# Expert weights in transfers of two units, 16 KB on a partition, over a ring of six pairs

## The chip, the core and the metric

The kernel runs on one core of one Trainium2 chip. What is measured is the device time of one execution in microseconds (us). Three runs of the kernel before took 1349.79, 1351.2 and 1353.6 us, a median of 1351.2 us.

## The reference

A decoder layer for 512 prompt tokens and 8 sample tokens. Its head (attention with a sliding window, a pooling mixer, a projection, norms) gives rows h of 1024 numbers. Its tail is a mixture of 32 experts, of which each token uses 4. Everything is float32.

```
logits = h @ w_router + b_router;  topv, topi = top_k(logits, 4);  gates = softmax(topv)
for every expert e and the tokens that chose it:
    gu = h[tok] @ w1[e] + b1[e]              # w1[e]: 1024 x 2048
    gate, up = gu[:, :1024], gu[:, 1024:]
    gate = min(gate, 7);  up = clip(up, -7, 7)
    act = (up + 1) * (gate * sigmoid(1.702 * gate))
    y[tok] += g * (act @ w2[e] + b2[e])      # w2[e]: 1024 x 1024
out = x + gate_ffn * y
```

An expert has 12 MB of weights (w1 8 MB, w2 4 MB), all 32 have 384 MB, and all are read from HBM once.

## The kernel before

The first 300 us are the head. After it come 32 passes, one expert each. `ORDER` gives every pass a class: A takes up to 256 token rows, B 128, C 64, D 32. The order is CCBBCBDDADDBBCCDADCBDDADCBCBCBDD: 3 passes of A, 9 of B, 9 of C and 11 of D. Experts with most rows get class A, and so on down. All passes read the same 12 MB whatever their class; what differs is the work of TensorE. In A and B it multiplies in three terms (`three`), for which ScalarE first makes a high part (`hi`, L2059) and VectorE a low part (`rawr`, L2242) of each half of a unit.

The weights of a pass are cut into 12 *units* of 1 MB, 8 KB on each of 128 partitions. Units 0 to 7 are w1, in which unit u holds rows 128u to 128u + 127; units 8 to 11 are w2, in which a unit holds 256 rows, two neighbouring rows on a partition. TensorE uses the units in the order of `pe_order()`: w1 of pass p, then w2 of pass p - 1 (in A these four stand between unit 3 and unit 4). Below, (p, u) is unit u of pass p. `unit_used` counts units that TensorE is done with, and each unit's place in that count is `USED`.

SyncE (SP) issues all weight transfers, one or two DMAs to a unit (two for w1 of A, whose halves of 512 columns are needed at different times; they have pieces of 2 KB). They go into `m.raw`, a ring of 13 slots of 1 MB (`RING`). Slots are handed on in the order of use: the transfer of a unit waits until the unit 13 places before it is used (`FREED`, `SLOT`), and it signals its slot's semaphore `raw_in`, on which TensorE (C, D) or ScalarE (A, B) waits. SP works strictly in order:

```
                if n >= RING:
                    sp.wait_ge(unit_used, USED[FREED[n - RING]])
                m.load_unit(sp, e[p], p, u)
```

At the start the 12 units of pass 0 and unit (1, 0) fill the ring while the head still runs, and units (1, 1) to (1, 4) go to four other buffers (`EARLY`), lent by tiles that are used later.

The rows of a pass come by an indirect DMA of GpSimd (POOL) and are turned on TensorE (`turn_x`, L2446): the transpose of columns 128k to 128k + 127 gives the left operand of unit k. The activations are turned by `turn_act` (L2470), with columns in steps of 2 (8 bytes), since a w2 unit has two neighbouring rows on a partition. The outputs of a pass go out by two indirect DMAs of POOL that add to HBM (yd at L1918, out_y_prompt at L1935); with more than one block of rows (A) there are four. Each waits for the one before of its kind.

Of the kernel before, what the change touches and what calls it, by code (L numbers as in the profile page):

```python
# [21 lines left out]
P = 128  # L22
# [78 lines left out]

def arrivals():

    total, at = [0] * RING, {}
    for unit in LOADS:
        total[SLOT[unit]] += 16 * unit_dmas(*unit)
        at[unit] = total[SLOT[unit]]
    return at, total
# [23 lines left out]
def build(nc, i, o):  # L132
    m = Record()
    m.i, m.o = i, o
    with ExitStack() as ctx:
# [162 lines left out]
        def et(name, shape, dt=F32):  # L298
# [23 lines left out]
                   for n, place in enumerate((aTl0, xTl0, hi0 + SLOT_B, hi0))}  # L322
        m.aTh = et("aTh", [P, 2 * KC, P], F32R)
# [52 lines left out]
def head(nc, m):  # L376
# [160 lines left out]

    def load_unit(sp, e, p, u):

        if (p, u) in EARLY:  # L540
            raw, landed = m.early[p, u][:], m.early_in
        else:
            raw, landed = m.raw[:, SLOT[p, u], :], m.raw_in[SLOT[p, u]]
        if u >= W1_UNITS:
            f = 2 * (u - W1_UNITS)
            src = w2[ds(e), f * P:(f + 2) * P, :].rearrange("e (p k) n -> p (e k n)", k=2)
            sp.dma_start(raw, src).then_inc(landed, 16)
        elif ORDER[p] == "A":
            j = u // 4
            for kk in range(2):  # L550
                k = 2 * (u % 4) + kk
                src = w1[ds(e), k * P:(k + 1) * P, :].rearrange("e p (h c) -> p (e h) c", h=2)
                sp.dma_start(raw[:, kk * D:(kk + 1) * D].rearrange("p (h c) -> p h c", h=2),  # L553
                             src[:, :, j * 512:(j + 1) * 512]).then_inc(landed, 16)
        else:
            src = w1[ds(e), u * P:(u + 1) * P, :].rearrange("e p n -> p (e n)")
            sp.dma_start(raw, src).then_inc(landed, 16)

    m.load_unit = load_unit
# [1153 lines left out]
def experts(nc, m):  # L1713
# [107 lines left out]
    with nc.Block() as block:  # L1821

        @block.sync
        def _(sp):
# [179 lines left out]
        def _(act):  # L2004
# [43 lines left out]
            def high_to(place):  # L2048

                while high_count[0] < len(SPLIT_UNITS) and USED[SPLIT_UNITS[high_count[0]]] <= place:  # L2050
                    n = high_count[0]
                    slot = SLOT[SPLIT_UNITS[n]]
                    act.wait_ge(m.raw_in[slot], ARRIVED[SPLIT_UNITS[n]])
# [364 lines left out]
        def _(pe):  # L2418
# [42 lines left out]
            def turn_act(c, h, before, lows):  # L2461
# [41 lines left out]
            def up_unit(c, u, raw, xT):  # L2503

                final = u == W1_UNITS - 1
# [3 lines left out]
                elif c == "C":  # L2509
                    for sec in range(2):  # L2510
                        for h in range(2):
                            last = mm(bank[sec][64 * h:64 * h + 64, :], xT[:, u % 4, 64 * (u // 4):64 * (u // 4) + 64],
                                      raw[:, D * sec + 512 * h:D * sec + 512 * h + 512], stop=final)
# [58 lines left out]
            def up_static(p, u):  # L2572
                if ORDER[p] in SPLIT:
                    split_unit(p, u)
                elif (p, u) in EARLY:
                    pe.wait_ge(m.early_in, len(EARLY) * 16)
                    up_unit(ORDER[p], u, m.early[p, u][:], m.xT[p % 2])
                else:
                    slot = SLOT[p, u]
                    pe.wait_ge(m.raw_in[slot], ARRIVED[p, u])  # L2580
                    up_unit(ORDER[p], u, m.raw[:, slot, :], m.xT[p % 2])

            def down(p):
# [7 lines left out]
                for u in range(W1_UNITS, UNITS):  # L2591
                    if c in SPLIT:
                        split_unit(p, u)
                    else:
                        slot = SLOT[p, u]
                        pe.wait_ge(m.raw_in[slot], ARRIVED[p, u])
# [168 lines left out]
```

## Time and profile before

| what | us |
|---|---|
| median of three runs | 1351.2 |
| the profiled execution, its own time | 1354.14 |
| its span, first to last instruction | 1352.6 |
| TensorE busy | 1218.1 |
| VectorE busy | 713.6 |
| ScalarE busy | 489.6 |
| GpSimd busy | 326.7 |
| mean granted clock of TensorE | 0.945 |

Times within the execution count from the start of its span. Busy time of TensorE is modelled: matmuls are pipelined, so "busy" is not "at its peak". The rows of the DMA engines are in the page's slices of 34 us each and in windows that are asked for; a share of 1.0 means that all 16 DMA engines moved packets all the time (a little over 1 can show where packets of one engine overlap). The time from the issue of a transfer to its landing contains its wait behind the transfers ahead of it in the queue.

### The profile page before, as it was taken

To read this page: it belongs to the slowest core of one execution; us is meant where nothing else is said; L and a number is where in the kernel's file an instruction comes from. 1 tells how busy PE (TensorE), PEld (TensorE's weight loads), DVE (VectorE), ACT (ScalarE), POOL (GpSimd) and SP (SyncE) were. 2 spreads that over 40 slices of the span, in tenths; PEclk is the share of its full clock that TensorE was granted. 3 is DMA by queue.
4 is the path that set the end of the run, shared out by engine and by line. 5 is a ranking of instruction groups with operands and counts; after the bars stand their busy time and mean duration, and the time that the engine had idled before them with its cause. 6 is when DMAs were issued, how large, how long until landed. Compare 5 with 4: busy or idle time off the path is not lost.

```text
span 1352.6 us, 17632 instructions
## 1 busy us (share of the span) xinstructions
PE 1218.1 (90%) x6408; PEld 725.9 (54%) x6408; DVE 713.6 (53%) x1118; ACT 489.6 (36%) x703; POOL 326.7 (24%) x353
## 2 busy tenths in 40 slices
PE   5899799969999979998899889998889998999973
PEld 2455455553675735755675247555457555565531
DVE  3532663463785874553794234546534536667530
ACT  5111432231564633332573133333323333546320
POOL 2232221031222213113322311143321133232111
PEclk9899799979999989999899999998979998999976
DMA  9950786489999999999999999999999999999993
GB/s 332 345 127 5 263 302 215 158 316 385 400 391 363 406 408 393 404 385 371 402 414 407 398 397 407 388 363 402 403 393 408 359 345 408 413 407 412 403 413 113
DMA packets 101404, 474.16 MB, mean 351 GB/s; under 512 B 17417, under 2 KB 19896, under 8 KB 55162
## 3 DMA queue, kind: packets, MB, share of 16 engines
q1 hardware_dynamic: 82282, 444.76, 82.2%
q0 software_dynamic: 18384, 26.53, 8.0%
q10 hardware_dynamic: 650, 1.72, 0.4%
q8 instruction: 52, 0.85, 0.3%
q14 instruction: 36, 0.29, 0.1%
HBM read 459.47 MB, written 32.66 MB: 364 GB/s over the span
## 4 chain that ended last, share of the span: by engine, by line
PE 53%; DMA 12%; DVE 6%; issue 4%; ACT 1%; POOL 1%; SPq 0%; POOLq 0%; DVEq 0%; ACTq 0%
PE bank L2422 51%; DMA raw<-in_w 5%; DVE rawr L2242 2%; DMA out_y_prompt<-gu,slot_tok 2%; DMA yd<-gu,idx_s 2%; DMA yd<-ost,idx_s 2%; PE bank L2470 1%; PE bank L2446 1%; ACT hi L2059 1%; POOL gu L1932 1%; DVE gu L2206 1%; DVE gu L2204 0%; DVE ost L2276 0%; ACT ost L2042 0%; SPq L553 0%
## 5 line engine op out<-in xcount | busy, mean ns | idle before, releaser
L2242 DVE TENSOR_TENSOR rawr<-raw,hi 128x1024 fp32r<-128x1024 f32 x288 | 351.6, 1263 | 106.3 <-ACT hi L2059 104.8
L2059 ACT CAST hi<-raw 128x1024 fp32r<-128x1024 f32 x288 | 294.8, 1048 | 166.1 <-PE bank L2422 140.9
L2422 PE MATMUL bank<-raw,xT_even 128*64 128x512 f32 (+1 forms) x704 | 135.2, 600 | 0.1
L1918 POOL DMA_INDIRECT yd<-ost,idx_s x31 | 56.5, 1824 | 325.4 <-ACT ost L2042 324.5
L2422 PE MATMUL bank<-raw,aT 128*32 128x256 f32 (+1 forms) x992 | 113.7, 478 | 11.5 <-DMA raw<-in_w 11.5
L2422 PE MATMUL bank<-raw,xT_odd 128*32 128x512 f32 (+1 forms) x544 | 84.8, 647 | 15.8 <-DMA raw<-in_w 15.8
L2422 PE MATMUL bank<-hi,xTh_odd 128*128 128x512 f32 x224 | 76.8, 426 | 19.8 <-DVE rawr L2242 19.5
L2422 PE MATMUL bank<-hi,aTh 128*128 128x512 f32 x240 | 77.3, 404 | 12.5 <-DVE rawr L2242 12.5
L2422 PE MATMUL bank<-hi,xTh_even 128*128 128x512 f32 x256 | 84.5, 412 | 3.9 <-DVE rawr L2242 3.8
L2204 DVE TENSOR_SCALAR gu<-bank 128x512 f32<-128x512 f32 (+1 forms) x50 | 31.4, 627 | 103.2 <-PE bank L2422 103.2
L2024 ACT ACTIVATE gu<-gu 128x512 f32<-128x512 f32 (+1 forms) x50 | 29.2, 583 | 145.6 <-DVE gu L2204 145.6
L2422 PEld LDWEIGHTS bank<-raw,aT 128*32 128x32 f32 (+1 forms) x992 | 42.2, 125 | 73.1 <-issue 40.6
L2422 PE MATMUL bank<-rawr,xTh_even 128*128 128x512 f32 x256 | 80.8, 397 | 0.0
L2422 PE MATMUL bank<-hi,xTl_even 128*128 128x512 f32 x256 | 80.8, 397 | 0.0
L1869 POOL DMA_DIRECT2D bt<-bd x32 | 18.6, 583 | 238.1 <-PE bank L2422 214.9
L2422 PE MATMUL bank<-hi,aTl 128*128 128x512 f32 x240 | 76.0, 399 | 0.0
L2422 PE MATMUL bank<-rawr,aTh 128*128 128x512 f32 x240 | 76.0, 399 | 0.0
L2422 PE MATMUL bank<-rawr,xTh_odd 128*128 128x512 f32 x224 | 72.7, 407 | 0.0
L2422 PE MATMUL bank<-hi,xTl_odd 128*128 128x512 f32 x224 | 72.0, 404 | 0.0
L2042 ACT ACTIVATE ost<-bank,slot_gate 128x512 f32<-128x512 f32 (+1 forms) x43 | 26.0, 634 | 123.9 <-PE bank L2422 112.1
L1935 POOL DMA_INDIRECT out_y_prompt<-ost,slot_tok x20 | 33.3, 1666 | 146.0 <-DVE ost L2276 143.2
L2422 PEld LDWEIGHTS bank<-raw,xT_even 128*64 128x64 f32 (+1 forms) x704 | 35.4, 126 | 60.4 <-issue 57.8
(387 smaller groups left out, 1847.6 us busy)
## 6 DMA issues: line engine op xcount, KB each, us to landing
raw<-in_w SPq DMA_DIRECT2D x356, 1024.0 KB, 14.7
raw<-in_w SPq DMA_DIRECT2D x48, 512.0 KB, 13.1
raw<-in_w_ada SPq DMA_DIRECT2D x21, 1024.0 KB, 7.7
w_in_sb<-in_w_in SPq DMA_DIRECT2D x4, 1280.0 KB, 16.2
w_out_sb<-in_w_out SPq DMA_DIRECT2D x4, 1024.0 KB, 9.0
early<-in_w SPq DMA_DIRECT2D x4, 1024.0 KB, 12.4
ada_more<-in_w_ada SPq DMA_DIRECT2D x3, 1024.0 KB, 13.8
xs<-in_x_prompt SPq DMA_DIRECT2D x4, 512.0 KB, 14.1
```

The costliest lines, as they stand in the source:

```text
L1869: gp.dma_start(m.bt[0:rows, buf, :], table[ds(e), :, :].rearrange("e r c -> (e r) c")).then_inc(bias_in[buf], 16)
L1918: gp.indirect_dma_start(yd_of[n], bass.IndirectOffsetOnAxis(ap=m.idx_s[:, p % 6, b:b + 1], axis=0), out_rows(p, b), None, bounds_check=lim ...
L1932: gp.tensor_tensor(scaled_rows(p, b)[rows, cols], out_rows(p, b)[rows, cols], g, ALU.mult).then_inc(wide_scaled, 1)
L1935: gp.indirect_dma_start(y_of[n], bass.IndirectOffsetOnAxis(ap=m.slot_tok[:, p % 6, b:b + 1], axis=0), scaled_rows(p, b), None, bounds_chec ...
L2024: nc.scalar.activation(gate, gate, ACT.Silu, scale=ALPHA).then_inc(silu_ready, 1)
L2042: done = nc.scalar.activation(out_rows(p, b)[:, n * w:(n + 1) * w], src, ACT.Copy, scale=m.slot_gate[:, p % 6, b:b + 1])
L2059: nc.scalar.copy(m.hi[:, (2 * n + h) % HI, :], m.raw[:, slot, h * D:(h + 1) * D]).then_inc(hi_done, 1)
L2204: v.tensor_scalar(gate, g, LIMIT, None, ALU.min).then_inc(gmin_ready, 1)
L2206: v.tensor_scalar(up, u, LIMIT, -LIMIT, ALU.min, ALU.max).then_inc(gu_free, 1)
L2242: v.tensor_tensor(m.rawr[slot][:, half], m.raw[:, slot, half], m.hi[:, (2 * n + h) % HI, :].bitcast(F32), ALU.subtract).then_inc(lo_done, 1)
L2422: return nc.tensor.matmul(out, lhsT, rhs, start=start, stop=stop, skip_group_check=True)
L2446: last = tr(bank[6][:, n * P:(n + 1) * P], xg[:, b, (k + n) * P:(k + n + 1) * P], m.ident[:])
```

## The change

Two neighbouring units make a pair, 2 MB, 16 KB on a partition. In most cases one DMA brings a pair. What moves:

- **Layout.** Partition p of a w1 pair holds rows 2p and 2p + 1 of its 256 rows, next to each other in HBM: one piece of 16 KB. A w2 pair of A, B and C holds rows 4p to 4p + 3 of its 512 rows, one piece of 16 KB. A w2 pair of D is one DMA of two pieces of 8 KB for each partition. The w1 units of A stay two DMAs each, in pieces of 2 KB.
- **Ring.** Pairs go round six pairs of slots, 0 to 11. Slot 12 holds unit (1, 0) once and is not used again. A pair waits until the *second* unit of the pair six places before it is used.
- **Landing.** One DMA has one semaphore, so both units of a pair wait for the whole pair (`LAND`).
- **Start.** Pass 0 and unit (1, 0) are loaded as single units, with the new layout. Unit (1, 5) becomes a fifth early unit, in two tiles of 4 KB.
- **Turns.** `turn_x` takes columns in steps of 2 (8 bytes) in place of neighbours; `turn_act` takes steps of 4 (16 bytes) in A, B and C, and stays at 2 in D.

The core of the diff:

```diff
-EARLY = [(1, u) for u in range(1, 5)]
-LOADS = [(0, u) for u in range(UNITS)] + [unit for unit in pe_order() if unit[0] and unit not in EARLY]
-FREED = [unit for unit in pe_order() if unit not in EARLY]
-SLOT = {unit: n for n, unit in enumerate(LOADS[:RING])}
-for after, unit in zip(FREED, LOADS[RING:]):
-    SLOT[unit] = SLOT[after]
+EARLY = [(1, u) for u in range(1, 6)]
+SINGLE = [(0, u) for u in range(UNITS)] + [(1, 0)]
+SLOT = {unit: n for n, unit in enumerate(SINGLE)}
+HELD = [(p, u) for p, u in pe_order() if not u % 2 and (p != 1 or u >= 6)]
+PAIRS = [unit for unit in HELD if unit[0]]
+FREED = {}
+for (q, w), (p, u) in zip(HELD, PAIRS):
+    FREED[p, u] = (q, w + 1)
+    SLOT[p, u], SLOT[p, u + 1] = SLOT[q, w], SLOT[q, w + 1]
...
+def one_transfer(p, u):
+    return ORDER[p] != "A" or u >= W1_UNITS
...
+    def load_pair(sp, e, p, u):
+        if not one_transfer(p, u):
+            load_unit(sp, e, p, u)
+            load_unit(sp, e, p, u + 1)
+            return
+        n = SLOT[p, u]
+        raw = m.raw[:, n:n + 2, :]
+        if u < W1_UNITS:
+            src = w1_pair(e, u // 2).rearrange("e (p k) n -> p (e k) n", k=2)
+        elif ORDER[p] == "D":
+            f = 2 * (u - W1_UNITS)
+            src = w2[ds(e), f * P:(f + 4) * P, :].rearrange("e (i p k) n -> p (e i) (k n)", i=2, k=2)
+        else:
+            src = w2_pair(e, (u - W1_UNITS) // 2).rearrange("e (p i k) n -> p (e i) (k n)", i=2, k=2)
...
+        sp.dma_start(raw, src).then_inc(m.raw_in[LAND[p, u]], 16)
...
-            for n in range(UNITS + 1, len(LOADS)):
-                p, u = LOADS[n]
+            for p, u in PAIRS:
...
-                if n >= RING:
-                    sp.wait_ge(unit_used, USED[FREED[n - RING]])
-                m.load_unit(sp, e[p], p, u)
+                sp.wait_ge(unit_used, USED[FREED[p, u]])
+                m.load_pair(sp, e[p], p, u)
...
-                    last = tr(bank[6][:, n * P:(n + 1) * P], xg[:, b, (k + n) * P:(k + n + 1) * P], m.ident[:])
+                    first = (k + n) // 2 * 2 * P
+                    last = tr(bank[6][:, n * P:(n + 1) * P], xg[:, b, first + n % 2:first + 2 * P:2], m.ident[:])
...
-                    first = 2 * P * (n // 2)
-                    last = tr(bank[7][:, n * P:(n + 1) * P], up[:, first + n % 2:first + 2 * P:2], m.ident[:])
+                    columns = up[:, n:2 * P:2] if c == "D" else up[:, n:4 * P:4]
+                    last = tr(bank[7][:, n * P:(n + 1) * P], columns, m.ident[:])
```

SP's order around the point where the w2 units of pass 9 end and the weights of pass 11 begin (`eid` holds the number of the expert; L547 and L557 are `load_unit`). The order names a semaphore by its first user in the program, so "bada_in" is `unit_used` here. Before:

```order
L547 ISA [waits bada_in]
L547 DMA raw_79<-in_w2 128x2048
L547 ISA [waits bada_in]
L547 DMA raw_79<-in_w2 128x2048
L1835 TENSOR_LOAD eid_210
L1835 ISA x2
L557 ISA [waits bada_in]
L557 DMA raw_79<-in_w1 128x2048
L557 ISA [waits bada_in]
L557 DMA raw_79<-in_w1 128x2048
```

And now, where L615 is `load_pair`:

```order
L615 ISA [waits bada_in]
L615 DMA raw_79<-in_w2 128x2x2048
L1893 TENSOR_LOAD eid_212
L1893 ISA x2
L615 ISA [waits bada_in]
L615 DMA raw_79<-in_w1 128x4096
```

One wait and one DMA stand where there were two of each; nothing changes its place among the passes.

TensorE's order in pass 15 (D), where its first w1 units are used (L2422 is `mm`, L2470 `turn_act`; `raw_in` is the landing of a slot). Before:

```order
L2422 MATMUL bank0<-raw_79,xT_odd_184 32x512 [waits raw_in3,vecs_in,us_tr]
L2422 MATMUL bank0<-raw_79,xT_odd_184 32x512 x3
L2422 MATMUL bank0<-raw_79,xT_odd_184 32x512 [waits raw_in4]
L2422 MATMUL bank0<-raw_79,xT_odd_184 32x512 x3
L2470 MATMUL bank7<-ident_49,gu_185 128x128 [waits gate_in,recip_ready,us_rows]
L2470 MATMUL bank7<-ident_49,gu_185 128x128 x3
L2422 MATMUL bank0<-raw_79,xT_odd_184 32x512 [waits raw_in5]
```

And now (L2479 and L2528 are the same two):

```order
L2479 MATMUL bank0<-raw_79,xT_odd_184 32x512 [waits raw_in2,vecs_in,us_tr]
L2479 MATMUL bank0<-raw_79,xT_odd_184 32x512 x3
L2479 MATMUL bank0<-raw_79,xT_odd_184 32x512 [waits raw_in2]
L2479 MATMUL bank0<-raw_79,xT_odd_184 32x512 x3
L2528 MATMUL bank7<-ident_49,gu_185 128x128 [waits gate_in,recip_ready,us_rows]
L2528 MATMUL bank7<-ident_49,gu_185 128x128 x3
L2479 MATMUL bank0<-raw_79,xT_odd_184 32x512 [waits raw_in4]
```

The instructions stand where they stood. What differs is that two units in a row wait for one landing.

## Rows read from the trace of the kernel before

**Rows 1.** The page: DMA engines in 40 slices of the span.
```profile
DMA  9950786489999999999999999999999999999993
GB/s 332 345 127 5 263 302 215 158 316 385 400 391 363 406 408 393 404 385 371 402 414 407 398 397 407 388 363 402 403 393 408 359 345 408 413 407 412 403 413 113
```

**Rows 2.** The waits of the whole span: us in total, times, longest us.
```profile
PEld bank L2422 <- DMA raw<-in_w: 46.1, 28, 4.7
```

**Rows 3.** The page, DMA issues: KB each, median us to landing.
```profile
raw<-in_w SPq DMA_DIRECT2D x356, 1024.0 KB, 14.7
```

**Rows 4.** The waits, 767 to 793 us.
```profile
PEld bank L2422 <- DMA raw<-in_w: 11.9, 8, 2.0
```

**Rows 5.** The waits, 970 to 995 us.
```profile
PEld bank L2422 <- DMA raw<-in_w: 13.3, 8, 2.5
```

**Rows 6.** The waits, 1303 to 1337 us.
```profile
PEld bank L2422 <- DMA raw<-in_w: 20.4, 11, 4.7
```

**Rows 7.** Windows: busy PE, PEld, DVE, ACT, POOL; clock, DMA share, GB/s.
```profile
610.00:620.00 10.00, 10.00 (x52) 6.74 (x50) 0.00 (x0) 2.07 (x4) 0.53 (x1) 1.00 0.84 318
880.00:890.00 10.00, 10.00 (x45) 5.34 (x45) 0.00 (x0) 2.81 (x5) 4.11 (x3) 1.00 0.83 323
...
1080.00:1090.00 10.00, 10.00 (x45) 7.71 (x45) 0.59 (x1) 0.73 (x2) 0.00 (x0) 1.00 0.78 314
760.00:770.00 10.00, 10.00 (x68) 3.09 (x62) 1.97 (x7) 1.28 (x2) 3.52 (x4) 1.00 1.02 420
```

**Rows 8.** SP's issues in time, 862 to 893 us: start, length, count.
```profile
868.00 11.32 SPq L547 DMA_DIRECT2D raw<-in_w  x3
884.49 6.88 SPq L557 DMA_DIRECT2D raw<-in_w  x4
```

**Rows 9.** Line L557, 884 to 886.5 us: from issue to landing.
```profile
DMA to landing us min/median/max: 5.0/5.0/5.0
```

**Rows 10.** Line L557, 748 to 757 us: from issue to landing.
```profile
DMA to landing us min/median/max: 20.4/20.6/24.0
```

**Rows 11.** DMA, 1290 to 1296 us: packets, MB, share of 16 engines.
```profile
DMA packets 352, 2.56 MB, mean 427 GB/s; under 512 B 39, under 2 KB 39, under 8 KB 39
...
q1 hardware_dynamic: 352, 2.56, 101.1%
```

**Rows 12.** DMA, 815 to 819 us.
```profile
DMA packets 693, 1.64 MB, mean 409 GB/s; under 512 B 44, under 2 KB 44, under 8 KB 643
...
q1 hardware_dynamic: 692, 1.63, 106.0%
```

**Rows 13.** DMA, 72 to 79.5 us.
```profile
q0 software_dynamic: 571, 1.45, 85.2%
q1 hardware_dynamic: 18, 0.15, 10.2%
```

**Rows 14.** TensorE in time, 773 to 800 us: start, length, operation, wait before.
```profile
777.07 1.06 PE L2422 MATMUL bank<-raw,xT_odd 128*32 128x512 f32 x8 [1.72 <-DMA raw<-in_w]
...
790.48 1.94 PE L2422 MATMUL bank<-raw,aT 128*64 128x512 f32 x8 [0.40 <-DMA raw<-in_w]
```

**Rows 15.** TensorE in time, 1300 to 1353 us: its last unit.
```profile
1335.59 1.07 PE L2422 MATMUL bank<-raw,aT 128*32 128x256 f32 x16 [0.91 <-DMA raw<-in_w]
```

**Rows 16.** Line L2446, turns of rows: ns min/median/max of one.
```profile
L2446 PEld LDWEIGHTS bank<-ident,xg_even x100: 137/141/223, 300.4 to 1258.7; 128*128 128x128 f32 x100
```

**Rows 17.** Line L2470, turns of activations.
```profile
L2470 PEld LDWEIGHTS bank<-ident,gu x178: 194/207/219, 322.8 to 1327.3; 128*128 128x128 f32 x178
```

**Rows 18.** ScalarE in time, 631 to 642 us.
```profile
640.91 0.47 ACT L2042 ACTIVATE ost<-bank,slot_gate 128x256 f32<-128x256 f32 x1 [7.97 <-POOL gu L1932]
```

**Rows 19.** The DMA view, issues of POOL: median us to landing.
```profile
out_y_prompt<-ost,slot_tok POOLq DMA_INDIRECT x20, 8.9
```

More of the change, by code:

```diff
@@ L99, in unit_dmas @@
     return 2 if u < W1_UNITS and ORDER[p] == "A" else 1
+def one_transfer(p, u):
+    return ORDER[p] != "A" or u >= W1_UNITS
+LAND = {unit: n for n, unit in enumerate(SINGLE)}
+for p, u in PAIRS:
+    LAND[p, u], LAND[p, u + 1] = SLOT[p, u], SLOT[p, u if one_transfer(p, u) else u + 1]
 def arrivals():
     total, at = [0] * RING, {}
-    for unit in LOADS:
-        total[SLOT[unit]] += 16 * unit_dmas(*unit)
-        at[unit] = total[SLOT[unit]]
+    for unit in SINGLE:
+        total[LAND[unit]] += 16 * unit_dmas(*unit)
+        at[unit] = total[LAND[unit]]
+    for p, u in PAIRS:
+        if one_transfer(p, u):
+            total[LAND[p, u]] += 16
+            at[p, u] = at[p, u + 1] = total[LAND[p, u]]
+        else:
+            for unit in ((p, u), (p, u + 1)):
+                total[LAND[unit]] += 16 * unit_dmas(*unit)
+                at[unit] = total[LAND[unit]]
     return at, total
@@ L322, in build @@
                    for n, place in enumerate((aTl0, xTl0, hi0 + SLOT_B, hi0))}
+        m.early[EARLY[4]] = [at(f"early4_{n}", [P, D], F32, place) for n, place in enumerate((x0 + 4096, aT0 + 4096))]
         m.aTh = et("aTh", [P, 2 * KC, P], F32R)
@@ L536, in tok, with w1_pair, w2_pair @@
         return slice(t * P, t * P + ROWS[t])
+    def w1_pair(e, j):
+        return w1[ds(e), 2 * j * P:2 * (j + 1) * P, :]
+    def w2_pair(e, j):
+        return w2[ds(e), 4 * j * P:4 * (j + 1) * P, :]
     def load_unit(sp, e, p, u):
+        j, one = u // 2 if u < W1_UNITS else (u - W1_UNITS) // 2, u % 2
+        if (p, u) == EARLY[4]:
+            for sec in range(2):
+                src = w1_pair(e, j).rearrange("e (p k) n -> p (e k) n", k=2)[:, one, sec * D:(sec + 1) * D]
+                sp.dma_start(m.early[p, u][sec][:], src).then_inc(m.early_in, 16)
+            return
         if (p, u) in EARLY:
@@ L542, in load_unit @@
         else:
-            raw, landed = m.raw[:, SLOT[p, u], :], m.raw_in[SLOT[p, u]]
-        if u >= W1_UNITS:
+            raw, landed = m.raw[:, SLOT[p, u], :], m.raw_in[LAND[p, u]]
+        if u >= W1_UNITS and ORDER[p] == "D":
             f = 2 * (u - W1_UNITS)
@@ L1829, in _ @@
             e = list(range(NE))
-            for n in range(UNITS + 1, len(LOADS)):
-                p, u = LOADS[n]
+            for p, u in PAIRS:
                 if p == PINNED and not u:
@@ L2052, in high_to @@
                     slot = SLOT[SPLIT_UNITS[n]]
-                    act.wait_ge(m.raw_in[slot], ARRIVED[SPLIT_UNITS[n]])
+                    act.wait_ge(m.raw_in[LAND[SPLIT_UNITS[n]]], ARRIVED[SPLIT_UNITS[n]])
                     for h in range(2):
@@ L2501, in down_bias, with up_unit @@
                 last.then_inc(bias_used, 1)
-            def up_unit(c, u, raw, xT):
+            def up_unit(c, u, raw, xT, halves=None):
+                if c == "C" and halves is None:
+                    halves = [raw[:, 0:D], raw[:, D:2 * D]]
                 final = u == W1_UNITS - 1
@@ L2512, in up_unit @@
                             last = mm(bank[sec][64 * h:64 * h + 64, :], xT[:, u % 4, 64 * (u // 4):64 * (u // 4) + 64],
-                                      raw[:, D * sec + 512 * h:D * sec + 512 * h + 512], stop=final)
+                                      halves[sec][:, 512 * h:512 * h + 512], stop=final)
                 else:
@@ L2575, in up_static @@
                 elif (p, u) in EARLY:
-                    pe.wait_ge(m.early_in, len(EARLY) * 16)
-                    up_unit(ORDER[p], u, m.early[p, u][:], m.xT[p % 2])
+                    pe.wait_ge(m.early_in, EARLY_LANDED)
+                    tiles = m.early[p, u]
+                    halves = [t[:] for t in tiles] if u == EARLY[4][1] else [tiles[:, 0:D], tiles[:, D:2 * D]]
+                    up_unit(ORDER[p], u, None, m.xT[p % 2], halves)
                 else:
                     slot = SLOT[p, u]
-                    pe.wait_ge(m.raw_in[slot], ARRIVED[p, u])
+                    pe.wait_ge(m.raw_in[LAND[p, u]], ARRIVED[p, u])
                     up_unit(ORDER[p], u, m.raw[:, slot, :], m.xT[p % 2])
@@ L2595, in down @@
                         slot = SLOT[p, u]
-                        pe.wait_ge(m.raw_in[slot], ARRIVED[p, u])
+                        pe.wait_ge(m.raw_in[LAND[p, u]], ARRIVED[p, u])
                         down_unit(c, u, slot)
```

18 lines of the change are left out of this document (13 added, 5 removed).

## The prediction

> **What bounds the kernel now.** I read the page's slices first. From 306 us on, after the head, the DMA engines are busy in nine tenths or more of nearly every slice, at 345 to 414 GB/s [rows 1]. The 32 passes have to bring 384 MB (402.7 million bytes). So the passes are close to the rate of the DMA engines, and TensorE's 90% of busy time is not the whole story. The question is when TensorE waits for a weight and when the weights wait for a slot.
>
> The waits answer it. TensorE's weight loads wait 46.1 us for expert weights in the whole span [rows 2], although a transfer is issued well ahead: 14.7 us pass in the median until it lands [rows 3]. By windows, 11.9 us of it lie in 767:793, 13.3 us in 970:995 and 20.4 us in 1303:1337 [rows 4 to 6], so nearly all of it in three stretches. In 777 us the wait stands before every unit [rows 14]. In between the weights are ahead. The windows of 10 us show the opposite state: at 610, 880 and 1080 us the DMA share falls to 0.84, 0.83 and 0.78, while TensorE is busy for the whole 10 us [rows 7]. These are the w2 units of the three A passes. A unit of A takes TensorE 5.5 us (the three issues from 868.00 on stand 5.5 us apart, then comes one at 884.49 [rows 8]) and a transfer far less, so the ring is full and the DMA engines stand idle. The time to landing says the same: 5.0 us for the transfer issued at 884.5, with nothing ahead of it in the queue [rows 9], and 20.4 us and more for those at 748 to 757, with several MB ahead of them [rows 10].
>
> So the tail is three cycles of one form. TensorE is the bound until the ring is last full (618, 884 and 1089 us, each time the end of an A pass); from there the DMA engines are the bound: TensorE uses up what is ahead, runs dry (near 770, 970 and 1303 us) and stays dry until the next A pass, or the end. In this part of a cycle TensorE's work is hidden, and two things count: how long the bytes take, and how far ahead the transfers were when the ring was last full.
>
> **The change part by part.**
>
> *Bytes in pieces of 16 KB.* The number of bytes stays. Between 1290 and 1296 us SP's queue moved 352 packets, 39 of them tiny (completions) and 313 of 8 KB, in 101.1% of 16 x 6.0 us, which is 97.1 us [rows 11]: 0.310 us for 8 KB with its share of the completions. Between 815 and 819 us it moved 692 packets in 106.0% of 16 x 4.0 us, 67.8 us; of them 44 are tiny, 599 have 2 KB and 49 have 8 KB [rows 12]. Less 49 x 0.310 us that leaves 52.6 us, 0.088 us for 2 KB. From 2 to 8 KB a packet grows by 0.222 us, so 8 KB more cost 0.296 us, and 16 KB would be 0.606 us against 2 x 0.310 us. Each engine has 8 partitions, so a pair costs 8 x 0.014 = 0.11 us less of some 4.96 us (2.2%). This counts only where DMA is the bound. In use order the last full moments lie at the issues of units number 128, 224 and 296, and the dry stretches end at 187, 259 and 383, so 60, 36 and 88 units lie between. Less the w2 units of D (4, 4 and 8), which keep pieces of 8 KB, that is 168 units or 84 pairs: 84 x 0.11 = -9.4 us. The bounds: nothing (16 KB cost just two of 8 KB), and 149 pairs in all of the tail x 0.11 = -16.4 us.
>
> The Trainium skill has a rule for this part (SBUF — State Buffer, "The DMA setup-cost knee"): a transfer pays about 2 us whatever its size, so a load that is bound by DMA should be merged into the largest transfers one can. By its formula (2 us + bytes / 436 GB/s) 1 MB takes 4.4 us and two units in one 6.8 us in place of 8.8; taken one after the other, 84 pairs would give back 168 us. The trace does not bear out that this cost is paid one transfer after the other: with several queued the engines moved 427 GB/s, 2.48 us to a unit [rows 11].
>
> *The ring, 12 slots in place of 13, freed two at a time.* When TensorE ended the A unit at 884.3 us, the transfer that could start was that of the unit 13 places later; all before it had landed or were nearly there. Now the last A unit is the second of its pair, and what its end frees is the pair six places later: units 11 and 12 places on. At the same moment the transfers are two units behind. That is the same at 618 and 1089 us, since all three are the end of unit (p, 11) of an A pass. Two units are 2 x 8 x 0.310 = 4.96 us of the DMA engines, and from there they are the bound, so nothing hides it: 3 x 4.96 = +14.9 us. It also adds up, since after each dry stretch TensorE is the bound and starts later. Bounds: one unit only for each cycle (+7.4 us) if a slot's reuse was late anyway, and three units (+22 us) if SP's wait for the second unit leaves a further hole. I take two, which the positions give.
>
> *Landing of pairs.* In a dry stretch TensorE now waits for 2 MB and then has two units to do. While it is dry that is hidden by the next transfer. At its end it is not: after the last landing two units stand before the end of the stretch, not one. A unit took 1.06 us at 777 us, 1.94 us at 790 us (the lower clock) and 1.07 us as the last of all [rows 14, 15]; I take 1.5 us, three times: +4.5 us (bounds 3 and 6).
>
> *SP.* It issues half as many DMAs and nothing changes place. Queued behind a waiting pair are only later pairs; no other queue is passed. Nothing.
>
> *Start.* Unit (1, 5) comes early, the first pairs of pass 2 come about when they did and the next ones some us later. No wait for weights before 767 us has any size (the three stretches hold 45.6 of the 46.1 us), so the cover is a deep one and I count nothing; if that cover were gone it would be one unit, 2.5 us.
>
> *Turns.* A weight load that turns neighbouring columns takes 141 ns, one with steps of 8 bytes 207 ns [rows 16, 17]. 178 loads of rows go from the first to the second: 178 x 66 ns = 11.7 us if all of it showed. Loads run beside matmuls and about half the tail is bound by DMA, so I take +1 us for all turns. The 16-byte step of 156 loads is not in the trace; by the nearest rows it lies between no change and twice 207 ns (0 to +32 us, or a little below nothing if the step does not matter). I take it as small, nearest to the step from 141 to 207 in a matmul stream that hides it. The Trainium skill (SBUF — State Buffer, "Door 1: The DMA port swizzle") says that SBUF has lines of 16 bytes and wants two hits or more in each. By that rule steps of 16 bytes, one hit in each line, are slower than steps of 8; the trace has only the two smaller steps, and already the one of 8 bytes costs 66 ns.
>
> **The sum.** -9.4 + 14.9 + 4.5 + 1 = +11.0 us, which I round down to +10, since a part of the extra idle time of the DMA engines lets POOL's transfers through, which they would have to carry anyway. On the profiled execution's own 1354.1 us that is 1364; it lies 2.9 us above the median of the runs, and on that median, 1351.2 us, the forecast is 1361 us.
>
> **The rivals.**
>
> *Larger pieces win.* The mechanism: the DMA engines are the bound all through, as the slices seem to say [rows 1], and the ring's last unit is never missed. Then the whole -16.4 us comes: 1335 us. For it speaks a share of 1.02 even at 760 us; against it the full ring at 610, 880 and 1080 us [rows 7]. The point from which it decides: the two lost units would have to cost under 1.5 us a cycle. The rule on merged transfers above points this way. Chance 0.15.
>
> *The two cancel.* The ring costs one unit a cycle: -9.4 + 7.4 + 3 = +1 us, 1352 us. Chance 0.15.
>
> *POOL's transfers get stuck behind large pieces.* At 640.9 us ScalarE had waited 7.97 us for the rows of an A pass to go out, and a store takes 8.9 us to land [rows 18, 19]. Its rows of 4 KB are 8 for an engine; if each waits for one weight packet, that packet grows from 0.31 to 0.61 us, +2.4 us for a store and +9.6 us for the four in a row after an A pass. That moves TensorE's stalls, and mostly where DMA is the bound and hides them; if all of it showed, 3 x 9.6 = +29 us beside the forecast's 10: 1390 us. Chance 0.07. That the engines take turns between queues by packets is what the Trainium skill says (DMA: Bandwidth & Descriptors, "Queues, rings and completion order").
>
> *Pieces of 16 KB are slow, or strides are.* Between 72 and 79.5 us SP's queue moved a load with 9 rows of 16 KB in 10.2% of 16 x 7.5 us: 1.36 us each, beside POOL's 85% [rows 13]. Were that the rate of such pieces alone, 149 pairs x 8 x 0.74 us = +880 us, 2230 us; I give it 0.01, since only the shared engines explain it as well. A piece 5% longer than forecast (0.636 us) gives 84 x 8 x 0.03 = +20 us beside the forecast's 10, 1381 us; the strides' full cost (+32 us) would give some 1392 us. Chance of these 0.07.
>
> **How the numbers follow.** Forecast 0.55, and the rivals 0.15, 0.15, 0.07 and 0.08. The range of the forecast itself, by the bounds of its ring and landing, is 1350 to 1369; to hold 8 in 10 it reaches toward the cases on both sides: 1344 to 1376 us. About 0.3% (4 us) is what a measurement can tell from no change. Faster by more: the first rival and a little of the second, 0.16. Within: the rest of the second and the low edge of the forecast, 0.16. Slower: 0.68.
>
> **What would show it.** Right: packets of 16 KB at about 0.606 us in a full stretch, near 430 GB/s; DMA shares below 0.8 at 610, 880 and 1080 us, lower than before; TensorE dry earlier than 767 and 970 us, with fewer and longer waits; about 5 us later at the first A pass after a dry stretch, about 8 at the next, 10 at the end. Wrong: no deeper idle of the DMA engines at the three full moments; or a rate in full stretches outside 420 to 435 GB/s; or new waits of TensorE for ScalarE or VectorE behind POOL's stores, or weight loads of L2528 well above 207 ns.

## The result, and the profile after

The changed kernel takes 1366.4 us in the median of 5 runs (1358.97 to 1369.26), the kernel before 1351.2: the ratio is 1.010, 95% interval [1.0067, 1.0133]. The forecast was 1361 us, its range 1344 to 1376. The profiled execution took 1358.97 us by its own time, the fastest of the five; its span is 1357.3 us at a mean granted clock of 0.951.

The page of the changed kernel, SP's queue and issues (packets, MB, share of 16 engines; then count, KB each, median us to landing), answers to [rows 3]:

```profile
q1 hardware_dynamic: 60618, 444.75, 81.3%
...
raw<-in_w SPq DMA_DIRECT2D x171, 2048.0 KB, 13.3
```

Of before the same row of the page is:

```profile
q1 hardware_dynamic: 82282, 444.76, 82.2%
```

The bytes are the same. The packets took 81.3% of 1357.3 us = 1103.5 us where they had taken 82.2% of 1352.6 = 1111.8 us.

The windows of the changed kernel (busy PE, PEld, DVE, ACT, POOL; clock, DMA share, GB/s), against [rows 7]:

```profile
610.00:620.00 10.00, 10.00 (x67) 4.87 (x65) 1.71 (x5) 2.80 (x5) 4.13 (x3) 1.00 0.69 256
...
880.00:890.00 10.00, 10.00 (x45) 6.46 (x46) 0.00 (x0) 2.42 (x4) 1.78 (x2) 1.00 0.53 183
...
1090.00:1100.00 10.00, 10.00 (x48) 4.14 (x48) 0.84 (x6) 2.80 (x5) 5.77 (x4) 1.00 0.73 256
```

At the end of each A pass the DMA engines stand idle longer than before: 0.69, 0.53 and 0.73 where it was 0.84, 0.83 and 0.78 (the third window lies 10 us later). A window of 10 us can cut such a hole in two, so these shares show that the holes are deeper and not by how many us.

The waits of TensorE's weight loads over the whole span of the changed kernel (us in total, times, longest):

```profile
PEld bank L2479 <- DVE rawr L2299: 56.1, 30, 10.4
PEld bank L2479 <- DMA raw<-in_w: 35.4, 13, 4.2
```

and of the kernel before, the row that [rows 2] does not show:

```profile
PEld bank L2422 <- DVE rawr L2242: 41.9, 27, 10.0
```

The wait for weights fell from 46.1 us in 28 waits to 35.4 in 13: fewer, and longer in the mean (1.6 to 2.7 us). That is not the whole wait for weights: in passes of A and B ScalarE takes them first (`hi`), and it waited 25.1 us in 8 waits before and 28.9 us in 12 in the changed kernel. The wait for VectorE's low parts rose by 14.2 us, of which 13.5 us lie behind the three A passes (14.7, 11.0 and 9.4 us in place of 10.0, 5.6 and 6.0). There it begins on POOL. These are the waits of POOL, of before, of the change and of the changed kernel with 8 KB pieces (e1_pieces8, below):

```profile
POOL gu L1932 <- DMA yd<-gu,idx_s: 26.7, 3, 9.5
```

```profile
POOL gu L1989 <- DMA yd<-gu,idx_s: 39.3, 3, 14.9
```

```profile
POOL gu L1983 <- DMA yd<-gu,idx_s: 26.9, 3, 10.1
```

POOL's second product of an A pass waits for its store; ScalarE waits for POOL, VectorE for ScalarE, TensorE for VectorE. In the changed kernel ScalarE's row that answers to [rows 18] is

```profile
643.24 0.47 ACT L2099 ACTIVATE ost<-bank,slot_gate 128x256 f32<-128x256 f32 x1 [11.47 <-POOL gu L1989]
```

11.47 us in place of 7.97. And the stores' landings (median us), against [rows 19]:

```profile
yd<-ost,idx_s POOLq DMA_INDIRECT x31, 10.9
...
out_y_prompt<-ost,slot_tok POOLq DMA_INDIRECT x20, 11.8
```

So a store takes 2.4 us more (8.5 before) and 2.9 us more (8.9 before). That is the third rival's mechanism, and it is real: behind the A passes TensorE's stalls are longer by it. Whether it costs time at the end is for the experiments.

Where the 13.5 us (1.0% of 1351.2) arise can be read from the semaphore on which TensorE counts units. From the first unit on (it is done at 303.8 us in the profiled run of before, at 296.8 in that of the change, and anywhere from 295 to 304 in the others, so spans alone mislead) the changed kernel is late, in us, after so many units:

```
units used           16   112   144   184   208   240   256   280   352   383
changed - before   +2.1  +3.5  +9.3 +11.5  +9.4 +14.4 +17.6  +9.9 +14.9 +13.9
12 slots - before   0.0  +2.4  +2.6  +6.6  +9.1  +9.7 +11.7 +12.4 +13.0 +14.8
```

(the second row is e3_ring12, below). The changed kernel jumps by about 5 us behind each A pass (units 112 to 144, 208 to 240, 280 to 352), where TensorE waits for VectorE, and gets a part back in the next dry stretch. The kernel that differs only in its ring gains nothing back. Each row is one execution: that of the change was the fastest of its five, that of e3 the slowest of its six, so the steps of a row say more than its end. In the dry stretches (184, 256, 383) the numbers also move by up to 3 us from one unit to the next, since the units of a pair land together.

### The profile page after: what moved, and what is told of

It is laid out like the page before. It is cut to its first block, busy times and chain, and to the rows that moved or that the text cites. A ratio compares the mean times of both kernels' runs of the same rounds, so it can differ in the third digit from the quotient of the medians.

```text
span 1357.3 us, 17126 instructions
## 1 busy us (share of the span) xinstructions
PE 1211.5 (89%) x6408; PEld 728.9 (54%) x6408; DVE 708.6 (52%) x1118; ACT 488.8 (36%) x703; POOL 322.4 (24%) x353
## 3 DMA queue, kind: packets, MB, share of 16 engines
q1 hardware_dynamic: 60618, 444.75, 81.3%
q10 hardware_dynamic: 650, 1.72, 0.4%
## 4 chain that ended last, share of the span: by engine, by line
PE 52%; DMA 14%; DVE 6%; issue 4%; ACT 1%; POOL 1%; POOLq 0%; SPq 0%; DVEq 0%; ACTq 0%
PE bank L2479 49%; DMA raw<-in_w 6%; DMA yd<-gu,idx_s 3%; DMA out_y_prompt<-gu,slot_tok 3%; DVE rawr L2299 3%; DMA yd<-ost,idx_s 2%; PE bank L2528 1%; PE bank L2504 1%; ACT hi L2116 1%; POOL gu L1989 1%; DVE gu L2263 1%; DVE gu L2261 0%; DVE ost L2333 0%; ACT ost L2099 0%; DMA out_y_prompt<-ost,slot_tok 0%
## 5 line engine op out<-in xcount | busy, mean ns | idle before, releaser
L2299 DVE TENSOR_TENSOR rawr<-raw,hi 128x1024 fp32r<-128x1024 f32 x288 | 347.3, 1250 | 115.7 <-ACT hi L2116 114.2
L2479 PE MATMUL bank<-raw,xT_even 128*64 128x512 f32 (+1 forms) x704 | 135.3, 600 | 0.1
L2479 PE MATMUL bank<-raw,aT 128*32 128x256 f32 (+1 forms) x992 | 113.9, 482 | 16.1 <-DMA raw<-in_w 16.1
L2479 PE MATMUL bank<-hi,xTh_odd 128*128 128x512 f32 x224 | 76.8, 426 | 34.1 <-DVE rawr L2299 34.1
L2479 PE MATMUL bank<-raw,xT_odd 128*32 128x512 f32 (+1 forms) x536 | 80.6, 631 | 11.4 <-DMA raw<-in_w 11.4
L2479 PE MATMUL bank<-hi,aTh 128*128 128x512 f32 x240 | 77.4, 404 | 12.7 <-DVE rawr L2299 12.7
L2479 PE MATMUL bank<-hi,xTh_even 128*128 128x512 f32 x256 | 82.5, 404 | 2.9 <-DVE rawr L2299 2.9
L2479 PEld LDWEIGHTS bank<-raw,aT 128*32 128x32 f32 (+1 forms) x992 | 43.7, 127 | 76.1 <-issue 44.5
L2479 PE MATMUL bank<-hi,xTl_even 128*128 128x512 f32 x256 | 79.6, 392 | 0.0
L2479 PE MATMUL bank<-rawr,xTh_even 128*128 128x512 f32 x256 | 79.6, 392 | 0.0
L2479 PE MATMUL bank<-rawr,aTh 128*128 128x512 f32 x240 | 75.5, 396 | 0.0
L2479 PE MATMUL bank<-hi,aTl 128*128 128x512 f32 x240 | 75.3, 395 | 0.0
L2479 PE MATMUL bank<-rawr,xTh_odd 128*128 128x512 f32 x224 | 72.6, 406 | 0.0
L2479 PE MATMUL bank<-hi,xTl_odd 128*128 128x512 f32 x224 | 72.5, 406 | 0.0
L2479 PEld LDWEIGHTS bank<-raw,xT_even 128*64 128x64 f32 (+1 forms) x704 | 35.4, 126 | 59.6 <-issue 54.9
```

The costliest lines, as they stand in the source:

```text
L2299: v.tensor_tensor(m.rawr[slot][:, half], m.raw[:, slot, half], m.hi[:, (2 * n + h) % HI, :].bitcast(F32), ALU.subtract).then_inc(lo_done, 1)
L2479: return nc.tensor.matmul(out, lhsT, rhs, start=start, stop=stop, skip_group_check=True)
```

## The experiments

Four kernels ran on each of three chips, each beside its own runs of the kernel before (medians 1349.8, 1351.55 and 1351.8 us). Ratios are against those; where two kernels of different chips are compared, their ratios are, and the intervals are combined as if independent.

**The change taken apart.** *e1_pieces8* keeps pairs, ring and joint landing, but moves every pair in pieces of 8 KB, with the layout and turns of before.

```
- src = w1_pair(e, u // 2).rearrange("e (p k) n -> p (e k) n", k=2)
+ src = w1[ds(e), u * P:(u + 2) * P, :].rearrange("e (i p) n -> p (e i) n", i=2)
```

> The changed kernel's ring, pairs, one DMA and one landing for a pair, but with the old layout: a pair comes in two pieces of 8 KB on a partition in place of one of 16 KB, and the turns take the columns as before. Theory 1 (the ring: transfers stand two units behind at each full moment): nothing of that changes, only the small gain of 16 KB pieces is lost, 84 x 8 x 7 ns = 5 us, so 1369 to 1373 us; the store of yd after pass 10 still holds GpSimd for 11 us. Theory 2 (POOL's stores wait behind pieces twice as long and hold ScalarE and then TensorE): the wait of GpSimd for the store of yd goes back from 11.3 to about 8.2 us, the step of 5 us in pass 11 disappears, and the time falls to 1352 to 1360 us.

1368.0 us, ratio 1.012 [1.0093, 1.0147]. That is 1 us below theory 1's range and far above theory 2's. POOL's wait is back at 26.9 us (the row above), its stores land in 8.5 us, and the kernel is not faster for it. So the stores' longer landing alone does not explain the loss; what may take its place here is said at e7.

*e2_two_dmas* is the changed kernel with each pair as two DMAs with a semaphore each.

```
- return ORDER[p] != "A" or u >= W1_UNITS
+ return False
```

> The changed kernel with its layout, turns and ring of six pairs, but every pair comes as two DMAs with a semaphore each (pieces of 8 KB). Against the run with 8 KB pieces in one DMA it differs in the landing alone. Theory 1: the ring's loss stays, the landing of pairs (my 4.5 us) goes away: 1361 to 1368 us. Theory 2: stores are short again and the ring costs little: 1351 to 1357 us.

1374.0 us, ratio 1.0189 [1.0163, 1.0215]: slower by more than any theory said. The two units of a pair land apart, TensorE waits 53.6 us in 33 waits, and the time is 9 us above e1's (from which it also differs by the layout and the turns, free by e4 below). So landing jointly costs nothing that shows here; why two DMAs for a pair cost more than one of the same pieces stays open.

*e3_ring12* is the kernel before with the 13th slot never used again; units are freed singly.

```
- FREED = [unit for unit in pe_order() if unit not in EARLY]
+ FREED = [unit for unit in pe_order() if unit not in EARLY and unit != (1, 0)]
```

> The kernel before with a ring of 12 slots in place of 13, freed one at a time (slot 12 holds unit (1, 0) once). Theory 1: one unit less at each of three full moments, 3 x 2.5 us: 1357 to 1360 us. Theory 2: the ring's length does not matter by itself, 1350 to 1353 us.

1362.4 us, ratio 1.0079 [1.0055, 1.0102], 10.7 us: above what was expected. One slot alone costs as much as three quarters of the change's loss. Its lateness begins at unit 92, long before the first dry stretch that the waits of TensorE had shown. There the first A pass begins, and it is ScalarE that waits. The first of its waits (2.8 us in three; the kernel before has none between 515 and 625 us), and TensorE's window 585:590 of before and of e3:

```profile
528.13 1.99 ACT L2059 CAST hi<-raw 128x1024 fp32r<-128x1024 f32 x2 [1.56 <-DMA raw<-in_w]
```

```profile
585.00:590.00 5.00, 5.00 (x38) 1.50 (x31) 2.19 (x9) 0.60 (x1) 2.31 (x4) 0.80 0.87 313
```

```profile
585.00:590.00 5.00, 5.00 (x25) 1.53 (x28) 2.05 (x5) 0.16 (x1) 1.90 (x3) 0.50 0.62 218
```

By the wait 1.1 us are lost at unit 92. The other 1.3 us are lost at units 104 to 106 with no wait: behind a short idle of TensorE that both kernels have, its granted clock is at the lower level (0.50, 1.2 GHz) for 6.8 us in e3, from 583.9 us on, and for 3.4 us in the kernel before.

*e4_layout* is the kernel before with the changed layout of weights and the turns by column steps.

```
- last = tr(..., xg[:, b, (k + n) * P:(k + n + 1) * P], m.ident[:])
+ last = tr(..., xg[:, b, first + n % 2:first + 2 * P:2], m.ident[:])
```

> The kernel before (13 single slots) with the changed kernel's layout of the weights (8 KB pieces at a pitch of 16 KB in HBM) and its turns with column steps of 2 and 4. Both theories: no change, 1350 to 1354 us. If the turns or the pitch carried a part of the loss it would be 1356 us or more.

1350.8 us, ratio 1.0012 [0.9992, 1.0031]: no change. The turn of activations in the changed kernel (ns min/median/max; the step is now 16 bytes for most), against [rows 17]:

```profile
L2528 PEld LDWEIGHTS bank<-ident,gu x178: 194/211/231, 317.6 to 1331.4; 128*128 128x128 f32 x178
```

**The ring against the pieces.** *e5_ring13_pairs* puts the 13th slot back and keeps 16 KB pieces wherever two slots are neighbours; *e8_ring13_pieces8* is the same with 8 KB pieces and the old layout; *e6_ring11* takes one slot more away; *e7_single_at_A* frees singly at the end of A passes.

```
e5:  for after, unit in zip(HELD, LATER):
         FREED[unit] = after
         SLOT[unit] = SLOT[after]
     ... one_transfer: SLOT[p, u + 1] == SLOT[p, u] + 1 and ...
e6:  - if unit not in EARLY]
     + if unit not in EARLY + [(1, 0), (0, 11)]]
e7:  if ORDER[q] == "A" and w >= W1_UNITS:
         for one in range(2):
             sp.wait_ge(unit_used, USED[q, w - 1 + one])
             m.load_unit(sp, e[p], p, u + one)
```

> Ring of 13 slots as in the kernel before, and 16 KB pieces: a pair goes as one transfer wherever its two slots are neighbours and it has 16 KB pieces (103 of 183 pairs); the other units go singly, each when its own slot is free. Theory 1 (what made the change slower is the lost slot and the freeing by twos at the full moments): a pair that waits for a slot 13 places back is issued at the end of an even unit, so next to nothing is missing at the full moments; the time is that of before less the gain of the larger pieces in the dry stretches, 0.11 us x about 47 pairs (103/183 of 84) = 5 us, plus at most 4.5 us of landing: 1345 to 1351 us, at least 10 us below the changed kernel. Theory 2 (large pieces cost as much as they give: stores of POOL land 2 to 3 us later, a pair lands later than its first unit): no gain from the ring, 1357 to 1366 us.

1353.8 us, ratio 1.0026 [1.0004, 1.0047]. With 13 slots, and pairs freed 13 places back, three quarters of the loss are gone, which theory 2 excludes; but the time lies 3 us above theory 1's range, so the pieces' 5 us, less the landing, did not come. Of all these kernels that keep the computation whole none beats the kernel before.

> The same issue order, pairs and ring of 13 as the run with 13 slots and 16 KB pieces, but every transfer in 8 KB pieces and the weights laid out as before. Theory 1 (a 16 KB piece is 0.014 us shorter than two of 8 KB, and this shows only in the dry stretches): 3 to 6 us above that run, 1350 to 1356 us. Theory 2 (a large piece gives nothing or less, since stores wait behind it): equal to that run within 2 us or below it.

1356.7 us, ratio 1.003 [1.0004, 1.0056]: against e5 0.04% more by the ratios (give or take 0.34%, 5 us), 2.9 us by the medians, too little to tell from none. The store of yd lands in 8.4 us here and in 10.1 us in e5.

> The kernel before with a ring of 11 single slots (the loads of the 12th and 13th slot are never followed by another), 8 KB pieces and single freeing as before. With 12 slots the ratio was 1.0079 [1.0055, 1.0102], 10.7 us. Theory 1 (each slot is a unit of head start lost at the full moments, linear): twice that, 1368 to 1374 us. Theory 1b (the first lost slot cost more than the prediction's 2.48 us a cycle for a reason of its own, and each further one costs 3 x 2.48 us): 1366 to 1369 us. Theory 2 (the last slots are spare, the loss with 12 slots was noise of the start): 1355 to 1362 us.

1375.5 us, ratio 1.0176 [1.0139, 1.0213], 23.8 us. The second slot costs 13 us, the first cost 10.7: linear, as theory 1 has it, and a little above its range.

> The changed kernel (12 slots, 16 KB pieces), but the two pairs that wait for the w2 units of an A pass (six pairs in all) go as single units, each when its own slot is free. Theory 1 (freeing by twos costs one unit at each of three full moments): 3 x 2.48 = 7.4 us less than the changed kernel, 1356 to 1361 us. Theory 2 (freeing by twos costs nothing, only the lost slot and the pieces do): within 2 us of the changed kernel, 1364 to 1368 us.

1363.2 us, ratio 1.0092 [1.0056, 1.0128]: 1 us below the changed kernel by the ratios, 3 by the medians, outside the range of either theory. The interval of the difference is some 7 us to either side, so the total alone just reaches the 7.4 of theory 1. Yet the hole at the end of the first A pass did close. The windows of e7_single_at_A show where it went:

```profile
610.00:620.00 10.00, 10.00 (x68) 4.92 (x67) 1.94 (x6) 2.81 (x5) 4.18 (x3) 1.00 0.95 369
660.00:670.00 10.00, 9.48 (x42) 7.55 (x41) 6.57 (x8) 5.16 (x6) 0.26 (x1) 0.91 0.86 305
...
880.00:890.00 10.00, 10.00 (x46) 6.45 (x46) 0.00 (x0) 2.42 (x4) 1.72 (x2) 1.00 0.77 296
920.00:930.00 10.00, 2.13 (x10) 1.41 (x8) 3.36 (x11) 2.33 (x3) 3.15 (x3) 0.73 1.03 404
930.00:940.00 10.00, 9.63 (x34) 7.79 (x35) 9.16 (x9) 4.47 (x5) 3.39 (x4) 0.76 0.89 326
```

The DMA share is 0.95 at 610 and 0.77 at 880 us (0.69 and 0.53 in the changed kernel). But then TensorE stands still behind POOL's stores (busy for 2.13 us in 920:930, 1.88 in 1130:1140), the transfers run on and fill the ring, and the share falls to 0.85 to 0.89 afterwards. The ring is last full there, not at the end of the A pass, and whatever was behind has been made up. The changed kernel has this second hole too (0.88 in 930:940, 0.89 in 1140:1150). The same window in it and in e1_pieces8:

```profile
930.00:940.00 10.00, 8.61 (x32) 7.04 (x33) 9.65 (x9) 4.40 (x5) 4.42 (x4) 0.76 0.88 353
```

```profile
930.00:940.00 10.00, 9.46 (x36) 7.70 (x37) 9.79 (x9) 4.49 (x5) 3.56 (x4) 0.83 1.03 407
```

The kernels with 8 KB pieces (before, e1, e3, e8) stall there as well, for less long, and have no second hole: their share stays at 1.01 or more. In e5, with 16 KB pieces and 13 slots, it is 0.94. So it takes the longer stall that the 16 KB pieces bring to fill the ring. In the changed kernel the stores' stall is paid and the freeing by twos hides beneath it; in e1 the stores are short and the freeing by twos can show, within the 5.5 us (give or take 5) that e1 lies above e3, which hold the landing and the start as well. That may be why e1 and the changed kernel take the same time. It is read from the shares; no run has the longer stall without the 16 KB pieces.

**Without the stall.** This reading was tested by leaving the stores of the A passes out, in four kernels: before, changed, e7's and e3's.

```
- gp.indirect_dma_start(yd_of[n], ...)
+ if c != "A":
+     gp.indirect_dma_start(yd_of[n], ...)
  ...
+ if c == "A":
+     continue
  gp.indirect_dma_start(y_of[n], ...)
```

(the waits on the two stores' semaphores count the remaining ones).

> The kernel before without the four stores that POOL issues for each of the three A passes (twelve in all; those rows are not added to the outputs). ScalarE then waits only for POOL's two products, and TensorE no longer stands still for 8 to 10 us after each A pass. All theories: faster than before, up to 3 x 9 us where TensorE is the bound, but the DMA engines are the bound behind it, so 5 to 20 us: 1330 to 1346 us. It is the base for the three runs beside it.

1335.9 us, ratio 0.9895 [0.9864, 0.9925]: 14.2 us faster than before.

> The kernel before with 12 single slots, without those twelve stores. Theory 1 (a lost slot is 2.48 us in each of four dry stretches, with or without the stall): 8 to 12 us above the kernel before without the stores. Theory 2 (the stall, during which the ring runs full, is what makes a slot cost 10.7 us and not 7.4): 4 to 7 us above it.

1349.0 us, 0.9988 [0.9966, 1.001]: 12.6 us above e9 by the ratios. A slot costs as much without the stall (a little over theory 1's range), and theory 2 falls, by little: the interval of the difference reaches from 7.5 to 18 us.

> The changed kernel with the same twelve stores left out. Theory 1 (in the changed kernel the hole that freeing by twos leaves at the end of an A pass is filled again while TensorE stands still behind POOL's stores; without the stores the hole stays open): the distance to the kernel before without those stores grows from 13.6 us to 17 to 22 us (7.4 for the slot, 7.4 for the twos, 4.5 landing, less 5 for the pieces, and a fourth dry stretch). Theory 2 (the stores' longer landing, 2 to 3 us each, is a part of the loss): the distance shrinks to 5 to 11 us. Theory 3 (stores and stall play no part): 11 to 16 us as with the stores.

1348.0 us, 0.9984 [0.9961, 1.0006]: 12.0 us above e9. The distance did not grow as theory 1 had it; by the total, theory 3 fits best, but the interval, 7 to 17 us, leaves the upper part of theory 2's range open. The parts moved, though:

> The changed kernel without those twelve stores, and with the six pairs that wait for w2 units of A passes sent as single units. With the stores this step gave 1 us at most. Theory 1 (the stall hid it): now it gives back the prediction's 3 x 2.48 = 7.4 us (5 to 9 us) against the changed kernel without the stores. Theory 3 (freeing by twos costs nothing whatever the stall): within 2 us of it.

1344.2 us, 0.9939 [0.9918, 0.9961]: 6.1 us below e10 by the ratios (3.8 by the medians; the intervals just meet), where the same edit with the stores gave 1 (3 by the medians). The two differ by 5 us, give or take 8, so the totals alone do not show that the stall hides the hole; the shares do. The windows of e11_single_no_stores and of e10_after_no_stores in the stretch behind the third A pass show no stall and no second hole:

```profile
1080.00:1090.00 10.00, 10.00 (x45) 4.90 (x43) 0.00 (x0) 2.80 (x5) 4.78 (x4) 1.00 0.79 292
...
1140.00:1150.00 10.00, 10.00 (x53) 3.86 (x51) 2.47 (x9) 1.78 (x3) 2.98 (x4) 1.00 1.01 412
```

```profile
1080.00:1090.00 10.00, 10.00 (x48) 3.94 (x49) 0.85 (x6) 2.80 (x5) 5.60 (x7) 1.00 0.74 251
...
1140.00:1150.00 10.00, 10.00 (x53) 3.90 (x51) 3.65 (x10) 2.06 (x4) 1.09 (x2) 1.00 1.01 402
```

The lateness by units against e9 (read as the table above):

```
units used           16    88   112   144   184   208   256   280   352   383
e12, 12 slots      +0.2   0.0  +2.3  +2.3  +5.8  +6.4  +9.4  +8.0  +8.0 +11.0
e10, changed       +2.4  +3.3  +7.1 +10.4 +13.4  +6.5 +13.1  +7.3  +7.9 +11.5
e11, singly at A   +2.4  +3.3  +7.0  +7.5  +9.1  +5.3 +11.6  +4.0  +4.6  +7.4
```

e12 loses 2.3, 4.1, 1.6 and 3.0 us in four places: the three dry stretches, and one at units 88 to 112. Against e11, e10 is 2.9 us later once the first A pass is over (unit 144), and 3.3 at 280, after the second cycle: in these two executions the step lies almost all at the first A pass, and not in three equal parts.

## Why the prediction came out right

The sign and the size were right, 1361 for 1366.4, but the size by terms that were off in both directions. That the sum came out within 6 us is in part luck. With the stores and, in brackets, without them:

| term | predicted | measured |
|---|---|---|
| one slot less | 7.4 | 10.7 [12.6] |
| freeing by twos at A | 7.4 | 1 [6.1] |
| pieces, landing, turns, start | -9.4 + 4.5 + 1 = -3.9 | +1.8 [-6.6] |
| all | 11.0 | 13.5 [12.0] |

Each measured term is a difference of two ratios. By their 95% intervals the first row is good to 3 us [5], the second to 7 [4], the third to 6 [4] and the last to 4 [5]. The third row is what remains: e7 less e3, and e11 less e12.

*What bounds the kernel.* Right: the ring is full at the A passes' ends, and what is missing there is not made up while the DMA engines are the bound. e3, e6 and e12 show that a lost slot costs, and costs linearly. Two things in the picture of three cycles were wrong.

*The slot, mis-sized: 7.4 us predicted, 10.7 and then 13.1 measured for the first and second slot.* The term took three dry stretches; the table of e12 shows a fourth place, units 88 to 112, where 2.3 us go. The step that failed is the reading of [rows 2]: it counted TensorE's waits alone, found all of the 46.1 us but 0.5 in three stretches, and took the cover before them for a deep one. But the ring is full a fourth time, at 330 to 340 us (DMA share 0.84 before, 0.67 in e3), and at 528 us the weights are ahead by less than one unit. With 12 slots ScalarE, which takes them there, waits 2.8 us. TensorE has lost 1.1 us by that and 1.3 us more by a lower granted clock (the windows of e3 above). Four places at 2.48 us would be 9.9 us; the four that were measured add up to 11.0. The granted clock is a part of the rest. In the runs of one and the same kernel 0.001 more of mean clock goes with about 0.7 us less; e3's runs have 0.942 in the mean where those of the kernel before beside them have 0.945, which is, as an estimate, 2 of its 10.7 us.

*Freeing by twos, 7.4 us predicted.* The hole came as predicted (0.69, 0.53, 0.73), but 1 us of it showed. The step that failed is the choice of the last full moment: [rows 18] had shown ScalarE held for 7.97 us behind POOL at 641 us, and the sum did not ask what the transfers do meanwhile. They fill the ring if the stall is long enough: behind the stalls of the kernel before they do not, behind those of the changed kernel (11.47 us here) they do. So this term and the third rival, the stores behind large pieces, were not to be priced apart: where the second comes, it can take the place of the first. Without the stores 6.1 us of the 7.4 appear.

*Pieces of 16 KB, -9.4 us predicted.* SP's queue in the changed kernel, 955 to 959 us, against [rows 11]:

```profile
DMA packets 139, 1.69 MB, mean 422 GB/s; under 512 B 36, under 2 KB 36, under 8 KB 36
...
q1 hardware_dynamic: 119, 1.69, 99.3%
```

1.69 MB are 103 pieces; 99.3% of 64 us by 103 is 0.617 us each with its share of completions, against 0.606 predicted and 2 x 0.310. Two other windows of 4 us, from 560 us (1.67 MB, 98.7%) and from 750 us (1.72 MB, 101.5%), give 0.62. Over the span the queue's packets took 8.3 us less (above), 0.056 us for each of 149 pairs, not 0.11; for 84 pairs that is -4.7 us. The slope from 2 KB to 8 KB was carried on to 16 KB and gave twice the gain. The Trainium skill's rule of a fixed cost of about 2 us for each transfer (SBUF — State Buffer, "The DMA setup-cost knee") would have made it 2 us a pair, and the trace again does not bear that out where transfers are queued.

*Landing of pairs, +4.5 us.* e1, with 8 KB pieces, is 0.41% or 5.5 us above e3, and e8 0.3% above before: pairs as such cost 4 to 6 us, which holds the landing, the twos and the start. e2 shows that it is not the joint landing as such, so this term had the right size at most by chance. The start, counted as nothing, makes 2.0 to 2.4 us by unit 16 in the changed kernel, e1, e5, e10 and e11, and at most 0.4 in e7 and e8, which have the same early units; the trace shows where: in these five the granted clock is 0.50 for 3.4 us between units 1 and 16 (in the changed kernel from 313.6 us on, 0.86 in 310:315 and 0.80 in 315:320), and in none of the others (e7: 1.00 in 310:315). TensorE was busy for 3.52 us of 310:315 in both kernels, so what decides whether the clock falls is open.

*Turns, +1.* Right, nothing measurable (e4). The Trainium skill's lines of 16 bytes (SBUF — State Buffer, "Door 1: The DMA port swizzle") would make steps of 16 bytes slower than those of 8; this trace has 211 and 207 ns.

*The rivals.* "Larger pieces win" falls with e5 and e8. "The two cancel" is excluded by the interval. The stores' latency came true to the size (+2.4 us a store) and added 12.6 us to POOL's waits (+9.6 us for each A pass, 29 in all, was the rival's price if all showed). e1 takes it away and does not gain, and the freeing by twos may come in its place. Without the stores in the A passes the third row of the table is 8.4 us better (give or take 7), which is the nearest to a price of the stall that these runs have. That the DMA engines take turns between queues by packets (the Trainium skill, DMA: Bandwidth & Descriptors, "Queues, rings and completion order") agrees with 8.5 us behind pieces of 8 KB and 10.9 behind 16 KB; no run looks at the turns themselves.

*What would show it.* The holes, the rate (422 GB/s) and the fewer waits came as said. But one of the signs of being wrong came too: new waits of TensorE for VectorE behind POOL's stores, +13.5 us behind the A passes. The sum had no term for them. TensorE did not run dry earlier: its first wait for weights before 800 us began at 771.9 us, and at 769.4 before, since it had itself been held up. "5, 8 and 10 us late" was 9.3, 9.4 and 9.9 at units 144, 208 and 280.

## What to carry to other kernels

Where a ring of buffers feeds a kernel that is bound by DMA in some stretches and by compute in others, a slot is worth one transfer in every place where the bound changes over, and those places are to be counted over every engine that takes from the ring, and by taking a slot away, not only by one engine's waits in one trace: a place where the cover is thinner than one transfer shows no wait yet. Before pricing a hole in the transfers, look whether the consumer stands still for another reason before the next dry stretch, and whether long enough to fill the ring: here stalls lengthened by the 16 KB pieces were, those beside 8 KB pieces were not. Larger pieces are not worth a slot when the transfers are queued anyway: here 16 KB in place of 8 KB gave under one per cent of the DMA time (8.3 of 1111.8 us), and made every small store of another queue 2.4 us longer.

## What was not expected of the hardware

Beside weight pieces of 8 KB a store of POOL lands in 8.5 us, beside 16 KB in 10.9 (both above; 8.4 and 10.1 in e8 and e5, which have the same ring). Weight loads that turn every second column take 207 ns and most with every fourth no more than 211. The first unit is done anywhere between 295 and 304 us in these profiled runs, although the code up to there is the same in most of them: more than half of what the change itself costs. The late ones (299 to 304 us) were at the lower granted clock for 41 to 48 us before that unit, those at 295 to 297 us for 34 to 38 us, with one exception (e12: 44 us and 297.0). And behind the same short idle of TensorE near 583 us the granted clock is at 1.2 GHz for 3.4 us in the kernel before and for 6.8 us in e3.
